# Three late modulation vectors summed on VectorE, through four half slots of the weight ring

## The reference, cut

```
mod_l = jnp.split((silu(c) @ w_ada + b_ada)[:, None, :], 6, axis=-1)
mod_c = jnp.split((silu(c_ctx) @ w_ada + b_ada)[None, None, :], 6, axis=-1)
n_lat = modulate(rmsnorm(h_lat, g_norm1), mod_l[0], mod_l[1])
n_ctx = modulate(rmsnorm(h_ctx, g_norm1), mod_c[0], mod_c[1])
h_lat = h_lat + mod_l[2] * mixer(n_lat, n_ctx)
f_lat = modulate(rmsnorm(h_lat, g_norm2), mod_l[3], mod_l[4])
h_lat = h_lat + mod_l[5] * peer_ffn(f_lat)
return rmsnorm(h_lat, g_final)
```

## Time and profile before

| what | value |
| --- | --- |
| time, median of 3 runs | 2512.51 us (lowest 2512.41) |
| the profiled execution's own time | 2509.06 us |
| its span | 2507.1 us |
| mean granted TensorE clock | 0.97 |
| busy: PE, DVE, ACT, POOL | 2094.7, 1197.7, 424.8, 1026.5 us |
| moved by DMA | 793.43 MB, mean 316 GB/s |

### The profile page before, as it was taken

One profiled execution on the slowest core, in us unless ns is written; L12 is line 12 of the kernel. 1 busy time (PEld: TensorE's weight loads), 2 busy tenths in 40 slices (PEclk: granted clock), 3 DMA queues, 4 the chain that ended last, 5 costly groups with the idle time before them and its releaser, 6 DMA issues.

```text
span 2507.1 us, 21137 instructions
## 1 busy us (share of the span) xinstructions
PE 2094.7 (84%) x8088; PEld 1169.3 (47%) x8088; DVE 1197.7 (48%) x1895; ACT 424.8 (17%) x812; POOL 1026.5 (41%) x881
## 2 busy tenths in 40 slices
PE   4699999999999797999688887777777777777777
PEld 1233333788888686878344432222222222222233
DVE  4614630156666111226654655466655766456441
ACT  4224420023333100010111011010111111110101
POOL 1010000569987001003644554555545555555541
PEclk9799999999999898999899999999999999999999
DMA  9987688934444457547999999999999999999995
GB/s 394 345 236 250 237 281 291 215 125 156 143 138 136 130 185 252 169 134 284 410 413 404 422 422 421 422 422 422 421 421 422 419 422 422 422 421 422 422 394 193
DMA packets 228419, 793.43 MB, mean 316 GB/s; under 512 B 25032, under 2 KB 144016, under 8 KB 148192
## 3 DMA queue, kind: packets, MB, share of 16 engines
q0 software_dynamic: 80832, 561.30, 55.1%
q1 hardware_dynamic: 137696, 225.55, 26.9%
q10 hardware_dynamic: 9792, 5.25, 0.7%
HBM read 778.36 MB, written 9.47 MB: 314 GB/s over the span
## 4 chain that ended last, share of the span: by engine, by line
DMA 34%; PE 17%; DVE 4%; POOL 3%; issue 2%; ACT 1%; DVEq 0%; ACTq 0%; POOLq 0%
DMA vb<-in_peer_v,eidx 30%; PE ps L1596 9%; PE ps L1543 5%; PE ps L1568 3%; DMA rows<-in_peer_u,eidx 2%; DMA mT<-in_peer_u,eidx 1%; POOL rows L1311 1%; POOL vb L1311 1%; POOL mT L1311 1%; DMA cut<-in_peer_sub_keys 1%; DVE rows L1503 0%; PE ps L1553 0%; PE ps L1578 0%; DVE oh L1464 0%; DVE oh L1466 0%
## 5 line engine op out<-in xcount | busy, mean ns | idle before, releaser
L1596 PE MATMUL ps<-vb,diag 128*128 128x512 f32 x2048 | 950.4, 611 | 291.2 <-DMA vb<-in_peer_v,eidx 286.7
L1596 PEld LDWEIGHTS ps<-vb,diag 128*128 128x128 f32 x2048 | 376.9, 192 | 862.2 <-DMA vb<-in_peer_v,eidx 453.1
L1311 POOL DMA_INDIRECT vb<-in_peer_v,eidx x256 | 370.1, 1446 | 493.4 <-PE ps L1596 476.1
L1503 DVE CUSTOM_DVE_ANT_0 rows<-rows,f 128x2048 f32<-128x2048 f32 x170 | 387.6, 2291 | 336.9 <-DMA rows<-in_peer_u,eidx 336.6
L1037 PE MATMUL ps<-nT,w_ring 128*128 128x256 f32 (+1 forms) x1792 | 522.8, 447 | 1.6 <-DVE nT L839 1.6
L1037 PEld LDWEIGHTS ps<-nT,w_ring 128*128 128x128 f32 x1792 | 336.1, 192 | 177.9 <-issue 141.3
L1503 DVE CUSTOM_DVE_ANT_0 mT<-mT,f 128x2048 f32<-128x2048 f32 x86 | 196.5, 2292 | 174.7 <-DMA mT<-in_peer_u,eidx 174.5
L1311 POOL DMA_INDIRECT rows<-in_peer_u,eidx x170 | 215.6, 1269 | 93.2 <-issue 48.8
L1387 ACT ACTIVATE diag<-ident,wgt 128x128 f32<-128x128 f32 x256 | 94.1, 397 | 661.5 <-PE ps L1596 656.2
L1311 POOL DMA_INDIRECT mT<-in_peer_u,eidx x86 | 104.4, 1214 | 211.9 <-DVE eidx L1473 163.9
L1008 PE MATMUL ps<-w_ring,scol 128*32 128x512 f32 x768 | 116.1, 687 | 45.1 <-DMA w_ring<-in_w_ada 45.1
(11 more groups left out here) (328 smaller groups left out, 1618.5 us busy)
## 6 DMA issues: line engine op xcount, KB each, us to landing
w_ring<-in_w_ada SPq DMA_DIRECT2D x96, 1024.0 KB, 5.7
w_ring<-in_w_in SPq DMA_DIRECT2D x56, 1024.0 KB, 5.6
w_ring<-in_w_out SPq DMA_DIRECT2D x16, 1024.0 KB, 5.5
w_ring<-in_peer_w_query SPq DMA_DIRECT2D x16, 1024.0 KB, 13.4
w_ring<-in_w_proj_a SPq DMA_DIRECT2D x8, 1024.0 KB, 5.5
w_ring<-in_w_proj_b SPq DMA_DIRECT2D x8, 1024.0 KB, 5.5
big<-big SPq DMA_DIRECT2D x128, 32.0 KB, 3.5
gates_dram<-gst POOLq DMA_DIRECT2D x16, 256.0 KB, 2.5
```

What stands on the lines that cost most here:

```text
L1311: pool.indirect_dma_start(ring[m % n], None, table, bass.IndirectOffsetOnAxis(ap=eidx[:, i % 3, j:j + 1], axis=0))\
L1503: v.tensor_tensor_reduce(ub[m % n_u], ub[m % n_u], f[:, i // HEADS], 1.0, 0.0, ALU.mult, ALU.add, hd[:, i % 2, j:j + 1]).then_inc(u_used, 1)
L1596: last = pe.matmul(ps[:, 4 * tile + c, :], diag[:, m % NDIAG], vb[m % NV][:, c * 512:(c + 1) * 512], start=(r == 0), stop=(r == HEADS * K ...
```

## The change

The late vector of chunk 2 stays on PE, now with four units in each of V's pairs (one behind every eighth k) and none in U. The other three (chunks 3, 4, 5) are summed on DVE: `mod_units` takes half units (128 rows x 1024 columns, 512 KB, 4 KB for each partition), multiplies each by one number per partition and adds it to `mod_sum[q]`, so that the 16 row blocks are added up elementwise in 96 instructions of 128x1024. PE then adds up the 128 partitions once for each vector (`row_sums`, four matmuls with a stationary tile of ones). The half units go through four half slots, which share ring slots 3 and 4 (`SHARED`); each is freed by DVE (`late_used`). `BESIDE` says how many loads SP issues beside each pair: in V four w_ada units, in U's pairs 20 half units each, in G's first two pairs 8 each; three quarters of them stand ahead of the second half of the next pair's weights. On DVE the 96 stand as 6 at each of the steps i = 8, 9, 10, then 38, then (behind Bb) 16, then 6, 6, 4, 4, 2, 2 ahead of G's units 0 to 5. The first sum lies in Bb, so POOL loads s5_b only behind `row_sums(1)` (after unit i = 13, U's sixth); the second lies in the gate weights' place, the third in PT. There is one tile mod_rows for all four vectors, outside gst, and the stores of the vectors stand at other places of POOL's list.

```diff
 FIRST_CHUNKS = (1, 0)
 LATE_CHUNKS = (2, 3, 4, 5)
+BESIDE = 4 * ((4, 0),) + 4 * ((0, 20),) + 2 * ((0, 8),)
+SUM_BEHIND = (13, 16, 22)
 UK = 8
 RING = 5
+HALF = D // 2
+SHARED = ((0,), (1,), (2,), (3, 5, 6), (4, 7, 8), (5, 3), (6, 3), (7, 4), (8, 4))
...
-        w_in_sem = [sem(f"w_landed{i}") for i in range(RING)]
+        w_in_sem = [sem(f"w_landed{i}") for i in range(len(SHARED))]
         units = []
-        freed_by, uses = [None] * RING, [0] * RING
+        freed_by, uses = [None] * len(SHARED), [0] * len(SHARED)
         def plan(src, slot, freed):
             uses[slot] += 1
-            units.append((src, slot, freed_by[slot], uses[slot]))
+            units.append((src, slot, [freed_by[x] for x in SHARED[slot] if freed_by[x] is not None], uses[slot]))
...
-        late = [(c, k) for c in LATE_CHUNKS for k in range(KD)]
+        late = [(c, k, x) for c in LATE_CHUNKS[1:] for k in range(KD) for x in range(2)]
+        late_at = []
+        def plan_late(count):
+            for _ in range(count):
+                n = len(late_at)
+                c, k, x = late[n]
+                src = t["w_ada"][0, k * P:(k + 1) * P, c * D + x * HALF:c * D + (x + 1) * HALF]
+                late_at.append(plan(src, RING + n % 4, (late_used, n + 1)))
...
-        ada_at += [plan_ada(*late[x], 3 + x) for x in range(2)]
-        for n in range(len(wide)):
-            plan_first(n + 1, turn[(2 * n + 2) % 3])
-            ada_at += [plan_ada(*late[8 * n + x], 3 + x % 2) for x in range(2, 8)]
-            plan_second(n + 1, turn[(2 * n + 3) % 3])
-            if n + 1 < len(wide):
-                ada_at += [plan_ada(*late[8 * n + 8 + x], 3 + x) for x in range(2)]
-        n_slot = [2]
+        for n in range(len(BESIDE)):
+            early, count = BESIDE[n]
+            for part in range(2):
+                for x in range((3 * early // 4, early - 3 * early // 4)[part]):
+                    ada_at.append(plan_ada(LATE_CHUNKS[0], len(ada_at) % KD, 3 + len(ada_at) % 2))
+                if part == 0:
+                    plan_first(n + 1, turn[(2 * n + 2) % 3])
+                plan_late((3 * count // 4, count - 3 * count // 4)[part])
+                if part == 0:
+                    plan_second(n + 1, turn[(2 * n + 3) % 3])
+        assert len(late_at) == len(late)
+        n_slot = [turn[(2 * len(BESIDE) + 2) % 3]]
         def next_slot():
             n_slot[0] = (n_slot[0] + 1) % RING
             return (n_slot[0] + RING - 1) % RING
-        for n in range(len(wide) + 1, len(pairs)):
+        for n in range(len(BESIDE) + 1, len(pairs)):
...
-            if freed is not None:
-                eng.wait_ge(freed[0], freed[1])
-            dst = w_ring[:, slot]
-            if len(src.shape) == 2:
+            for s, count in freed:
+                eng.wait_ge(s, count)
+            dst = slot_view(w_ring, slot)
+            if len(src.shape) == 2 and slot < RING:
...
+def slot_view(w_ring, slot):
+    if slot < RING:
+        return w_ring[:, slot]
+    whole, half = divmod(slot - RING, 2)
+    return row_view(w_ring[:, 3 + whole])[:, half * HALF:(half + 1) * HALF]
...
+        mod_rows = big[:, 13888:14400]
+        mod_sum = [Bb.rearrange("p r g h -> p (r g h)"), mT[:, KW:KD, :].rearrange("p k n -> p (k n)"),
+                   PT.rearrange("p b r g n -> p (b r g n)")]
@@ gpsimd @@
-            pool.wait_ge(acc_free, V0 + 2)
-            for r, name in enumerate(("s5_b_re", "s5_b_im")):
-                for d in range(2):
-                    pool.dma_start(Bb[d * N:(d + 1) * N, r], t[name][0, d].rearrange("g n h -> n g h"))\
-                        .then_inc(b_in, 16)
+            def load_b():
+                pool.wait_ge(late_sum, 1)
+                for r, name in enumerate(("s5_b_re", "s5_b_im")):
+                    for d in range(2):
+                        pool.dma_start(Bb[d * N:(d + 1) * N, r], t[name][0, d].rearrange("g n h -> n g h"))\
+                            .then_inc(b_in, 16)
             def store_mods(q):
                 pool.wait_ge(mod_free, NFIRST + q + 1)
-                rows = mod_rows[0:P:32, q % 2]
                 at = LATE_CHUNKS[q] * D
-                pool.dma_start(mods_dram[0, at:at + D].rearrange("(j n) -> j n", j=4), rows).then_inc(mods_out[q % 2], 16)
-            store_mods(0)
+                pool.dma_start(mods_dram[0, at:at + D].rearrange("(j n) -> j n", j=4), mod_rows[0:P:32])\
+                    .then_inc(mods_out, 16)
             for k in range(KW):
-                if k % 4 == 0:
-                    store_mods(1 + k // 4)
                 pool.wait_ge(acc_free, U0 + k + 1)
                 pool.dma_start(u_dram[k], zu[:, k % 2]).then_inc(u_out, 16)
+                if k == 0:
+                    store_mods(0)
+                if k == SUM_BEHIND[0] - KW:
+                    load_b()
+                    store_mods(1)
                 pool.wait_ge(u_out, 16 * (k + 1))
-            store_mods(3)
...
             imaginary_product(0)
             build_pb(0)
+            store_mods(2)
             for s in range(NSTAGE + 2):
                 if s + 1 < NSTAGE:
                     imaginary_product(s + 1)
                 if s < NSTAGE:
                     rotations(s)
+                if s == 0:
+                    store_mods(3)
@@ scalar @@
             def late_rows(q):
-                act.wait_ge(ada_used, KD * (NFIRST + q + 1))
-                if q >= 2:
-                    act.wait_ge(mods_out[q % 2], 16 * (q // 2))
-                act.activation(mod_rows[:, q % 2], ps[:, 6 + q % 2, :], ACT.Copy).then_inc(mod_free, 1)
+                if q == 0:
+                    act.wait_ge(ada_used, KD * (NFIRST + 1))
+                else:
+                    act.wait_ge(late_sum, q)
+                    act.wait_ge(mods_out, 16 * q)
+                act.activation(mod_rows, ps[:, 6 + q % 2, :], ACT.Copy).then_inc(mod_free, 1)
...
-                if i and i % 4 == 0:
-                    late_rows(i // 4 - 1)
...
-            late_rows(NLATE - 1)
+                if i == KW:
+                    late_rows(0)
+                if i == SUM_BEHIND[0]:
+                    late_rows(1)
...
+                if 2 * KW + k in SUM_BEHIND:
+                    late_rows(SUM_BEHIND.index(2 * KW + k) + 1)
@@ vector @@
+            late_n = [0]
+            def mod_units(count):
+                for _ in range(count):
+                    n = late_n[0]
+                    late_n[0] += 1
+                    q, k, x = n // (2 * KD), n // 2 % KD, n % 2
+                    if n == 2 * KD:
+                        v.wait_ge(g_full, 4 * KW)
+                    w = unit(v, late_at[n])
+                    total = mod_sum[q][:, x * HALF:(x + 1) * HALF]
+                    if k == 0:
+                        ins = tsc(total, w, scol[:, k, 0:1], None, ALU.mult)
+                    else:
+                        if x == 0:
+                            v.wait_ge(late_used, n)
+                        ins = stt(total, w, scol[:, k, 0:1], total, ALU.mult, ALU.add)
+                    ins.then_inc(late_used, 1)
             for i in range(KW + 3):
                 if i < KW:
                     conv(i)
...
                     q_of(i - 2)
                 if i >= 3:
                     scans(i - 3)
+                if i >= KW:
+                    mod_units(6)
+            mod_units(38)
...
             v.wait_ge(bb_ready, 2)
+            mod_units(16)
             for b in range(2):
                 v.wait_ge(kz_full, b + 1)
...
             for k in range(KW):
+                mod_units((6, 6, 4, 4, 2, 2, 0, 0)[k])
                 v.wait_ge(acc_free, G0 + k + 1)
@@ tensor @@
-            def late_units():
-                q, k = divmod(ada_n[0] - NFIRST * KD, KD)
-                if k == 0 and q >= 2:
+            def row_sums(q):
+                pe.wait_ge(late_used, 2 * KD * q)
+                if q >= 2:
                     pe.wait_ge(mod_free, NFIRST + q - 1)
-                ada_unit(6 + q % 2)
+                for j in range(4):
+                    last = pe.matmul(ps[32 * j:32 * j + 32, 6 + q % 2, :], notfirst[:, 1:33],
+                                     mod_sum[q - 1][:, j * 512:(j + 1) * 512], start=True, stop=True)
+                last.then_inc(late_sum, 1)
...
-                        if beside is not None and k % 4 == 3:
-                            beside()
+                        if beside is not None and k % UK == UK - 1:
+                            beside(6)
                     yield
...
-                for _ in columns(V0 + 2 * c, 0, 2 * T, late_units):
+                for _ in columns(V0 + 2 * c, 0, 2 * T, ada_unit if i < KW else None):
                     if 1 <= i <= KW:
                         gates(i - 1)
+                    if i == SUM_BEHIND[0]:
+                        row_sums(1)
                     i += 1
             lag_zero()
             for c in range(KW // 2):
                 for _ in columns(G0 + 2 * c, T, 2 * T):
```

(26 more changed lines are left out.)

7 lines of the change are left out of this document (3 added, 4 removed).

## The result

| | before | after |
|---|---|---|
| median | 2514.34 us (4 runs) | 2560.66 us (2559.01 to 2562.06, 4 runs) |
| span of the profiled execution | 2507.1 | 2556.8 |
| mean granted TensorE clock | 0.97 | 0.951 |
| w_ada groups on PE | 768 matmuls | 384 |

The ratio is 1.0187, with a 95% interval of 1.0167 to 1.0207: 46 us slower, where I had forecast 11.5 and a range that ended at 2560. Slower is shown; whether by more than 2% is not, as the interval has 2% in it. One of the four runs before took 4359.79 us, far off the other three, and is left out of the ratio.

What follows compares the result with a forecast made beforehand. PE was taken to bound the kernel until G's end. S starting 34.4 us later, less 22.9 gained in V, made 11.5 us more: 2509.1 + 11.5 + 3.4 = 2524 us, range 2480 to 2560.

Steps and rivals of the forecast that it cites:

- step 2: U's later pairs: half units turn in 1.3 us, 31 us a pair, stalls of 6.3 and 2.8 us.
- step 3: Ahead of G: s5_b, Bb, 15 half units and weights beside the copies make G0 start at 185 for 164.7.
- What is removed: V and U: w_ada units leave PE; V gains 22.9 us with its stall, U loses 35.5 us of work.
- Step 1: U's second pair: its late weights, issued at 44.5, land at 51.0, so PE stalls for 15.8 us.
- Step 4: G: stalls of 6.2 and 3.4 us, row sums and slow starts add 14.1 us to 57.0.
- The sum: Whole kernel: 34.4 us later at S less V's 22.9 is 11.5 us more, giving 2524 us.
- (d): Rival, U and G's approach: half units turn in only 1.6 us and copies halve the rate; 2564 us; 10%.
- (c): Rival, half-unit loads: bytes bind at 349 GB/s, 1.50 us a half unit; 2542 us; 12%.
- (b): Rival, U and G's approach: first stall stays, half units turn in 1.26 us, copies cost nothing; 2484 to 2500 us; 18%.

Runs made afterwards that it cites:

- x_bytes: The changed kernel with each half unit loading 512 of its 1024 columns (256 KB for 512 KB); 2532.5 us, ratio 1.0079 to the kernel before.
- x_nodve: The changed kernel with VectorE's multiply-adds run over 8 columns of 1024, loads unchanged; 2539.1 us, ratio 1.0113 to the kernel before.
- x_nocopies: The changed kernel with the 32 copies from u_dram carrying 1/16 of their bytes; 2539.9 us, ratio 1.0112 to the kernel before.

## Why the prediction was wrong

The direction and the chain were right; terms of the sum were too small. Two of them failed: the turn of the half slots in U (step 2), and the price of the copies' company for the half units and the weights (step 3). Two smaller ones are s5_b and the slow starts. Against the prediction's own marks:

| mark (r) | predicted | measured |
|---|---|---|
| V's gain | 22.9 | 24.3 |
| DVE at L0 | 21.6 | 21.6 |
| U's second pair starts | 51.0 | 52.4 |
| U's third pair | 85.5 | 92.2 |
| U's fourth pair | 116.5 | 135.9 |
| U's end | 144.7 | 166.0 |
| `lag_zero`'s end | 156.6 | 174.6 |
| G0 starts | 185 | 214.9 |
| G's end | 256.1 | 296.5 |

**What is removed** was right: V gained 24.3 us less 1.1 us of a later start, 23.2, for 22.9.

**Step 1** held: DVE's place (21.6), q_of(7) (28.8 for 29.2), the issue of the late load (44.35 for 44.5), and the wait (16.9 for 15.8). DVE's marks came from rows of its order, which the change leaves as it is; the load landed in 8.0 us for my 6.5.

**Step 2** failed in the size of the turn. I had bounded a half unit between 1.3 and 1.6 us and took 1.3 "as the bytes are halved for certain". Between 355.5 and 393.6 us 20 half units and two w_in loads landed, by bytes 24 half units: 1.6 us each, and so 3.2 for a w_in load for my 2.5. A load landed in 5.2 us (6.0 in the third pair), no sooner than a whole unit in the earlier trace rows, not in the 3.9 that I had got by taking bytes off: four slots turn in (5.2 + 1.3) / 4 = 1.6. An account that fits is that four half units in flight share the DMAs as two whole ones did. x_bytes (3.3 us) and x_nodve (34 us a pair) show both terms of that turn. It cost 5.3 us in U's third pair (1.0 of it in the w_in load's landing) and 12.7 more in the fourth, about half of it by s5_b's loads beside, as that pair's load took 14.3 us to land for my 6.5. For G0 only the lateness of `row_sums(1)` counts directly, 8.1 us; U's end sets when the copies begin. The Trainium skill's fit (DMA: Bandwidth & Descriptors, Anatomy of one DMA), which gave 1.1 us a turn, is off here: it is for one load issued by GpSimd, and these are SP's, in company. Its rule to batch to 1 MiB isn't tested, as no run sends whole units to VectorE.

**Step 3** failed in the company of the copies. `lag_zero` started at U's end, which had passed Bb's time. G0 started 29.9 us late, and the table of its way gives the parts: 8.1 from U, 3.6 for s5_b (28.6 us for 25), 6.8 for the 15 half units (33.4 for 26.6), and 11.4 for the weights, whose landing took 21.3 for my 10, outside my bounds of 7.6 to 16.6. The last two are the copies' company: without the copies they took 26.4 and 8.0 (x_nocopies). The trace before had a warning that I passed over. From 455 to 475 us, beside the copies, its DMAs were full at 140 GB/s, a third of the 414 of the opening, where I had counted with half speed at worst:

```profile
455.00:475.00 20.00, 20.00 (x89) 17.44 (x88) 3.35 (x5) 0.77 (x2) 19.83 (x34) 0.94 1.07 140
```

**Step 4** was 10.5 short (81.6 for 71.1): waits of 17.6 for 9.6, and slower starts. The granted clock was 0.54 in the 40 us of the wait and 0.88 in G, for 0.97 before; a pair in U took 29.2 to 30.1 us for the 28.2 that I had counted, behind each wait. That PE's clock falls from the higher of its two levels (1.2 and 2.4 GHz) to the lower when PE stands idle is what the Trainium skill says (TensorE: Matmul & The Clock Gate, Part 1), and the trace agrees: 0.54 is near the lower level. I had counted slow starts for G and not for U, 4.4 us.

**The sum.** 40.4 us late at G's end: 8.1 + 3.6 + 6.8 + 11.4 + 10.5. The end was 36.7 above the forecast, as V gained 0.3 more, the stretch behind G was 1.7 shorter, and the median stood 1.7 above the profiled execution for my 3.4. Of the rivals (d) came nearest, at 2564: 1.6 us a half unit and copies that halve the rate. I had given it 10%, as there was "no company in most of U"; its own company, four slots deep, was enough. That its total is so near is in part luck: it adds 18 us in U, 20 in step 3 and 2 in G, and 8.1, 21.7 and 10.5 were measured. (c) is out with its 349 GB/s: in x_nodve the same loads moved 383 GB/s in U, over the 358 of the Trainium skill too (DMA: Bandwidth & Descriptors, Where 436 GB/s comes from). But it has a point: at 383 the DMAs were full, so the 414 of the opening weren't to be had here, and part of the 1.6 us may be bytes. (b) was also priced wrongly: with G0 at 168 for 185 and G as in step 4 the sum gives 2524 - 17 = 2507, not 2484 to 2500.
